# One 512-column product for two weight chunks in the input projection of an attention stage

## The reference

```python
xn = rms_norm(x, norm_g[i])
proj = jnp.einsum('bsd,de->bse', xn, w_in[i])
qa, ka, va, za, qb, kb, vb, zb = jnp.split(proj, cuts, axis=-1)
# q, k: rms_norm per head of 64
# 4 differential heads: dense softmax of two scores, a = softmax(s1) - lam * softmax(s2), o = a v, rms_norm
# 8 neighbourhood heads on a 16 x 64 grid: softmax over an 8 x 16 window with a relative bias, o = p v
ya = oa * jax.nn.silu(za);  yb = ob * jax.nn.silu(zb)
y = jnp.einsum('bse,ed->bsd', jnp.concatenate([ya, yb], axis=-1), w_out[i])
```

## Time and profile before

| | |
|---|---|
| three runs | 3197.17, 3199.08, 3201.27 us |
| median | 3199.08 us |
| span of the profiled execution | 3193.0 us |
| PE busy | 3109.5 us, 97% |
| PEld busy | 2705.6 us, 85% |
| DVE busy | 2028.7 us, 64% |
| POOL busy | 1420.3 us, 44% |
| ACT busy | 1058.5 us, 33% |

### The profile page before, as it was taken

One profiled execution on the slowest core, in us unless ns is written; L12 is line 12 of the kernel. 1 busy time (PEld: TensorE's weight loads), 2 busy tenths in 40 slices (PEclk: granted clock), 3 DMA queues, 4 the chain that ended last, 5 costly groups with the idle time before them and its releaser, 6 DMA issues.

```text
span 3193.0 us, 51486 instructions
## 1 busy us (share of the span) xinstructions
PE 3109.5 (97%) x19108; PEld 2705.6 (85%) x19108; DVE 2028.7 (64%) x3766; ACT 1058.5 (33%) x2057; POOL 1420.3 (44%) x1207
## 2 busy tenths in 40 slices
PE   9999999999989999999999999999999999999998
PEld 8898989988987889888888888988889888888886
DVE  4757576665788212687777775455553777777766
ACT  3545454541124210422222221544341422222221
POOL 5434344316643334665555545411104755555534
PEclk9999999999999999999999999999999999999999
DMA  7211201143112112111111111000002011111111
GB/s 199 75 56 38 67 28 54 38 172 97 67 34 63 52 45 68 38 59 47 53 53 53 53 53 63 7 21 17 18 21 93 27 53 53 53 53 53 53 52 53
DMA packets 181828, 179.58 MB, mean 56 GB/s; under 512 B 50234, under 2 KB 163066, under 8 KB 181498
## 3 DMA queue, kind: packets, MB, share of 16 engines
q1 hardware_dynamic: 181566, 177.02, 17.4%
q10 hardware_dynamic: 96, 0.26, 0.0%
HBM read 160.12 MB, written 22.38 MB: 57 GB/s over the span
## 4 chain that ended last, share of the span: by engine, by line
PE 63%; DVE 2%; issue 1%; ACT 1%; POOL 0%; POOLq 0%; DVEq 0%; ACTq 0%
PE banks L2692 16%; PE banks L79 13%; PE banks L81 13%; PE banks L80 13%; PE banks L3509 2%; PE banks L3486 1%; PE banks L215 1%; PE banks L3443 0%; PE banks L3444 0%; PE banks L3425 0%; POOL x L183 0%; PE banks L3452 0%; PE banks L2314 0%; DVE x L2929 0%; POOL rstd L178 0%
## 5 line engine op out<-in xcount | busy, mean ns | idle before, releaser
L2929 DVE TENSOR_TENSOR x<-x,banks 128x512 f32<-128x512 f32 x784 | 523.2, 687 | 242.2 <-PE banks L2692 233.7
L79 PE MATMUL banks<-winbuf_hi,xt_hi 128*128 128x256 f32 x1024 | 302.2, 295 | 11.7 <-ACT qkn L933 5.5
L80 PE MATMUL banks<-winbuf_lo,xt_hi 128*128 128x256 f32 x1024 | 290.0, 283 | 0.0
L81 PE MATMUL banks<-winbuf_hi,xt_lo 128*128 128x256 f32 x1024 | 290.0, 283 | 0.0
L79 PEld LDWEIGHTS banks<-winbuf_hi,xt_hi 128*128 128x128 f32 x1024 | 196.1, 191 | 33.5 <-issue 13.0
L79 PE MATMUL banks<-h1t_hi,f1w_buf_hi 128*128 128x512 f32 x512 | 199.5, 390 | 1.6 <-issue 1.6
L79 PE MATMUL banks<-h3t_hi,f2w_buf_hi 128*128 128x512 f32 x512 | 199.5, 390 | 1.6 <-issue 1.6
L81 PE MATMUL banks<-h3t_hi,f2w_buf_lo 128*128 128x512 f32 x512 | 199.2, 389 | 0.0
L81 PE MATMUL banks<-h1t_hi,f1w_buf_lo 128*128 128x512 f32 x512 | 199.2, 389 | 0.0
L80 PE MATMUL banks<-h1t_lo,f1w_buf_hi 128*128 128x512 f32 x512 | 199.2, 389 | 0.0
L80 PE MATMUL banks<-h3t_lo,f2w_buf_hi 128*128 128x512 f32 x512 | 199.2, 389 | 0.0
(11 more groups left out here) (545 smaller groups left out, 9339.6 us busy)
## 6 DMA issues: line engine op xcount, KB each, us to landing
f1w_raw<-in_w_ff SPq DMA_DIRECT2D x32, 1024.0 KB, 5.1
f2w_raw<-in_w_ff SPq DMA_DIRECT2D x32, 1024.0 KB, 5.1
winraw<-in_w_in SPq DMA_DIRECT2D x128, 128.0 KB, 3.3
gluw_raw<-in_ssm_w_glu SPq DMA_DIRECT2D x14, 512.0 KB, 4.6
x<-in_x SPq DMA_DIRECT2D x8, 512.0 KB, 6.3
wow_raw<-in_w_out SPq DMA_DIRECT2D x4, 1024.0 KB, 5.9
x<-in_x SPq DMA_DIRECT2D x1, 4096.0 KB, 15.2
gew_raw<-in_w_ple_gate SPq DMA_DIRECT2D x4, 1024.0 KB, 4.8
```

The costliest lines, as they stand in the source:

```text
L79: nc.tensor.matmul(out, a.hi, b.hi, start=start, stop=False)
L80: nc.tensor.matmul(out, a.hi, b.lo, start=False, stop=False)
L81: return nc.tensor.matmul(out, a.lo, b.hi, start=False, stop=stop)
L2929: nc.vector.tensor_tensor(xx, xx, chip.ps[:, 4 + 2 * (p % 2) + g, :], ALU.add).then_inc(s_acc, 1)
```

## The change

Two chunks can now go through one product of 512 columns into the whole of bank 6: the moving operand takes one 256-column row from each of two buffers, the output is two halves. The list `ROUNDS` says which chunks and which token tile a round has. There are 72 rounds: 8 single ones of chunk 0, 4 of chunk 1 (tiles 0 to 3), 4 pairs of chunks 1 and 2 (tiles 4 to 7), and one round for each step of units 0 to 6: for t below 4 the pair (2u + 2, 2u + 3), from t = 4 on the pair (2u + 3, 2u + 4); in unit 6 the last four are chunk 15 alone. So the heads of a unit are projected four tiles earlier than its values.

In a step the first projection is gone; the round stands where the second one was, between `scores(g + 2)` and `values(g)`. At t = 7 `scores(g + 1)` moves behind `transposes(g)`. On ACT `taken` takes both halves; it moves behind `down(g + 2)` and the second exp, and `squares(g)` moves with it behind both. The head sums, roots and scales, before eight tiles in steps 0 to 3, come one per step, three tiles ahead. There are three weight buffers instead of two, and no `winraw` of its own: the raw chunk lands in the low half of its pair and is split there in place. The next load of a buffer waits for the last round that reads it. Half of the unnormalised heads of odd units get a place of their own.

```diff
+    ROUNDS = [((0,), j) for j in range(NT)] + [((1,), j) for j in range(4)] + [((1, 2), j) for j in range(4, NT)]
+    for u in range(NU - 1):
+        for t in range(NT):
+            pair = (2 * u + 2, 2 * u + 3) if t < 4 else (2 * u + 3, 2 * u + 4)
+            ROUNDS.append((tuple(c for c in pair if c < 2 * NU), t))
+    def pair_rows(cs, k):
+        a, b = sorted(c % 3 for c in cs)
+        hi = m.win_hi[:, 16 * a + k:16 * b + k + 1:16 * (b - a), :]
+        first, last = (Mixers.LOWS[n] - Mixers.LOWS[0] + k for n in (a, b))
+        return Pair(hi, m.win_lo[:, first:last + 1:last - first, :])
...
+            def weights(c):
+                if c >= 2 * NU:
+                    return
+                if c >= 3:
+                    sp.wait_ge(s_p, last_round(c - 3) + 1)
+                for piece in range(4):
+                    for h, col in enumerate(columns(c)):
+                        sp.dma_start(m.raw[c % 3][:, 2 * piece:2 * piece + 2, h * P:h * P + P],
+                                     w_in[:, 2 * piece:2 * piece + 2, col:col + P]).then_inc(s_win[c % 3][piece], 16)
...
             for u in range(NU):
                 for t in range(NT):
-                    g, n = NT * u + t, 2 * NT * (u + 1) + 2 * t
+                    g = NT * u + t
                     more = u < NU - 1
-                    if more:
-                        project(n)
-                        if t == 7:
-                            scores(g + 1)
-                    elif t < 7:
+                    if not more and t < 7:
                         keep_going(t, 3)
-                    else:
+                    elif not more:
                         begin_output(0)
                     transposes(g)
                     if t < 6:
                         scores(g + 2)
                     if more:
-                        project(n + 1)
+                        if t == 7:
+                            scores(g + 1)
+                        project(PROLOGUE + g)
...
+            def taken(r):
+                cs, j = ROUNDS[r]
+                act.wait_ge(s_p, r + 1)
+                for c in sorted(cs):
+                    src = banked(cs, c) if len(cs) == 2 else chip.ps[:, 6, 0:CH]
+                    (values_taken if c % 2 else heads_taken)(c // 2, j, src)
...
                     more = u < NU - 1
-                    if more:
-                        taken(n)
                     evacuate(g)
...
                     if t < 7:
-                        if more:
-                            taken(n + 1)
                         if t == 1 and u and UNITS[u - 1][0] == "D":
                             out_hi(u - 1, 1)
                         if t == 4 and UNITS[u][0] == "D":
                             out_hi(u, 0)
                         if t < 6:
                             expo(g + 2, 0)
+                            down(g + 2)
+                            expo(g + 2, 1)
+                        if more:
+                            taken(PROLOGUE + g)
                         squares(g)
                         if more and t in (5, 6):
                             head_hi(u + 1, 2 * (t - 5))
                             head_hi(u + 1, 2 * (t - 5) + 1)
-                        if t < 6:
-                            down(g + 2)
-                            expo(g + 2, 1)
...
+            head_sums(NT)
+            head_sums(NT + 1)
+            head_scale(NT)
+            head_sums(NT + 2)
+            head_scale(NT + 1)
             biased(0)
+            head_scale(NT + 2)
             combine(0)
             biased(1)
```

More of the change, by code:

```diff
@@ L447, in stage_mixers @@
         s_xin = sems(nc, ctx, "mxx", " ".join(str(j) for j in range(NT)))
-        s_win = sems(nc, ctx, "mxw", "0 1 2 3")
+        s_win = [sems(nc, ctx, f"mxw{b}", "0 1 2 3") for b in range(3)]
         s_sst = sems(nc, ctx, "mxst", "0 1 2 3")
@@ L512, in _ @@
             sp.dma_start(m.xgain[:, :], row_bcast(io["norm_g"])).then_inc(s_xg, 16)
-            for piece in range(4):
-                weights(piece)
+            weights(0)
             for j in range(1, NT):
@@ L527, in _ @@
             sp.dma_start(io["s_rpb"], m.wide[:, :]).then_inc(s_wide, 16)
-            for piece in range(4, 8):
-                weights(piece)
+            weights(1)
             sp.wait_ge(s_bv, 4)
@@ L533, in _ @@
             spread_strip(sp, 0)
-            for piece in range(8, 12):
-                weights(piece)
+            weights(2)
             strips(0)
+            weights(3)
             sp.wait_ge(s_wide, 16)
@@ L542, in _ @@
             for u in range(NU - 1):
-                for t in range(4):
-                    weights(4 * (2 * u + 3) + t)
+                weights(2 * u + 4)
                 if u:
@@ L548, in _ @@
                     edges(0)
+                weights(2 * u + 5)
                 if u < NU - 2:
-                    for t in range(4):
-                        weights(4 * (2 * u + 4) + t)
                     sp.wait_ge(s_add, 2 * (NT * u + NT))
                     (strips if UNITS[u][0] == "D" else edges)(UNITS[u][1] + 1)
-            sp.wait_ge(s_p, 2 * NT * NU)
+            sp.wait_ge(s_p, len(ROUNDS))
             sp.wait_ge(s_split, 8 * NU)
@@ L1239, in _ @@
                         finish(g - 1)
-                    if more and t < 4:
+                    if a < NT * NU:
                         head_sums(a)
-                    if more and 1 <= t <= 4:
-                        head_scale(a - 1)
                     if more and t == 7:
@@ L1268, in _ @@
                             gated(u, 0)
-                    if more and t < 4:
+                    if a < NT * NU:
                         head_scale(a)
-                        head_sums(a + 1)
                     if dense:
```

127 lines of the change are left out of this document (74 added, 53 removed).

## The result

| | before | after |
|---|---|---|
| median | 3198.12 us (4 runs, 3196.95 to 3201.27) | 3286.55 us (4 runs, 3285.94 to 3287.31) |
| ratio | | 1.0278, 95% interval 1.0264 to 1.0293 |
| span of the profiled execution | 3193.0 us | 3285.1 us |
| TensorE's mean granted clock | 0.994 | 0.984 |
| standstills of PE over 1 us, 60 to 900 us | 9, together 16.9 us | 39, together 89.4 us |

What follows compares the result with a forecast made beforehand. PE's own order was taken to set the end, others counting only where PE stands. Prologue 9.4, N units 18.6 and D units 8.0 gave +36.0 on a 3193.0 span, 3229.0; plus 6.1, 3235 us; range 3212 to 3258.

Steps and rivals of the forecast that it cites:

- the mechanism: PE's loop steps: score transposes (T) lose the 2.9 us projection ahead of them, so their unchanged waits become bare.
- the N unit's standstills: Grid (N) units 1, 3, 5: PE stands before the transposes; +6.2 us per unit, +18.6 in all.
- what costs nothing: Weight splits, weight DMAs, in-place buffers, loads and head sums, roots and scales: forecast to add nothing.
- the ring: Dense (D) units: finish, combine, bias, exp, down, exp, taking, squares, variance, root, finish; 10.3 to 10.8 us against PE's 9.85.
- the width: Projection: one 512-column matmul instead of two 256-column ones saves 13.5 ns per pair, 18.1 us in all.
- those of 1 us left the clock at 1.00: Argument against the clock falling after PE's standstills, a part of rival 2.
- Rival 2: 3255 us: ring at its upper value costs each D unit 5 more, or the clock goes down, +6.5 to +34; chance 0.16.
- so four steps hide it: D units: the ring may fall behind, since combine(g+1) is needed only some 4.6 us after it is done.
- The D unit: Dense units: 89.4 us against 87.19 for units 2 and 4, +2.2 each; all D units together +8.0.
- The prologue: Before the loop and step 0: four pair rounds replace four single ones, +10.2; with the other terms +9.4 together.
- unit 0: First dense unit, from its T(1) on: 79.0 us against 74.7, +4.3.
- unit 6: Last dense unit with rounds, single from t = 4, 11.5 us less on PE: 81.4 us against 82.1, -0.7.

Runs made afterwards that it cites:

- e4: Changed kernel with each wide round split, k-tiles 0 to 3 ahead of the transposes, 4 to 7 behind the scores, and ScalarE's old order: 3178.53 us, 0.9945.
- e9: e4 with squares and head_hi on ScalarE behind both exps, the taking still early: 3211.65 us, 1.0044.
- e6: e4 with 256-column products, the first chunk's 24 ahead of the transposes, the second's 24 behind the scores: 3190.72 us, 0.9982.
- e5: Changed kernel with short groups of small filler matmuls in PE's standstills to keep the clock up: 3265.56 us, 1.0217.
- e3: Changed kernel with the round's taking, squares and head_hi of D units ahead of the second exp on ScalarE: 3267.79 us, 1.0222.
- e12: Changed kernel with e5's fillers and e3's ScalarE order together, with 8 fillers at t = 5 of D units: 3252.80 us, 1.0175.
- e7: e4 with the whole round ahead of the transposes, nothing between scores and values, and the taking ahead of evacuate: 3205.49 us, 1.0029.
- e10: e4 with the whole round ahead of the transposes in N units at t = 0 to 5 and D units at t = 0, 1, 3, 4: 3177.10 us, 0.9940.
- e11: e4 with the whole round ahead of the transposes in N units at t = 0 to 5 only: 3175.39 us, 0.9933.

## Why the prediction was right or wrong

**Right: the mechanism and the N unit's standstills.** T lost its cover, the unchanged waits became bare, and all seven units have T(6) and T(7) waiting on qklo. Forecast against measured in N units: T(2) 3.0 and 2.8, T(3) and T(4) 0.6 and 0.5, T(5) 2.2 and 2.0, T(6) and T(7) 1.9 and 1.99. e4 gives half the cover back, together with ScalarE's old order; e9, which keeps squares late, is still 75 us below the kernel after. So lost cover, with the clock that its standstills cost, is the main cause.

**Right: what costs nothing.** Buffers, loads, splits and head work cost nothing: e4 has them all and PE hardly stands. Only when the ring is late does a split hold PE up (e9).

**Right in kind: the width.** Forecast 18.1 us, measured 12.2 (e6 against e4). The 0.2257 us a wide matmul was read too low: the 443 of the window include those that overlap its ends, and between starts it is 0.2267 (441 starts in 99.73 us). By that the saving would be (0.2392 - 0.2267) x 24 x 56 = 17 us. Another part goes at the start of a group of wide matmuls, where the first distance is 0.33 us and the next four are 0.228 to 0.236 (the round from 311.95: 5.34 us over 23 distances), against 0.22 and then 0.12 in a narrow one. The transition that one projection fewer should have saved, 0.1 us a step, did not come. The rule of the Trainium skill that I had set against the rows ("TensorE: Matmul & The Clock Gate", Back-to-back issue gap) states, for a single matmul, a spacing of columns / 2.4 GHz plus about 2.5 ns; by it the change would save an estimated 3.4 us. It does not hold for these matmuls: they are 0.2267 us apart, not 0.216, and the narrow ones 0.1196, not 0.109.

**Wrong: the clock, "those of 1 us left the clock at 1.00".** I knew a drop after 3.54 us and no drop after 1.12, and most of the forecast's standstills are of 1.9 to 3 us, between the two. I put them with the short ones, without a reason. The trace of the kernel before had the warning behind the mixers: PE's standstill of 2.24 us ending at 1053.62 (L2314) was followed by 3.4 us at half clock, one of 2.05 us ending at 1031.44 was not:

```profile
1054.47:1057.88 3.41, 3.41 (x14) 3.12 (x13) 2.67 (x4) 2.13 (x4) 0.00 (x0) 0.50 0.97 272
```

The drop did come: 16 stretches, six of them behind one of the 13 standstills of 2.0 us. My own price of 1.6 us per drop was right (1.5 in N units); the number of drops was the error. e5 measures 21 us. Rival 2 held this cause at +6.5 to +34 and the ring at 5 us per D unit, but gave them as alternatives ("or the clock goes down") and at 0.16. Both happened.

**Wrong: the ring, "so four steps hide it".** The working had the right members, sized them at 10.3 to 10.8 us, and then counted on 4.6 us of slack. A turn measured 11.5 us (squares at 347.15 and 358.62): from `finish` (349.24) to the bias (353.01) it takes 3.8 us and not at most 3.3. The D unit, measured from T(0) in unit 2:

| | forecast | after | e5 (clock kept) |
|---|---|---|---|
| T(0) to T(4) | 39.9 | 45.5 | 45.5 |
| to T(5) | 12.8 | 13.1 | 13.2 |
| to T(6) | 15.5 | 16.8 | 16.8 |
| to T(7) | 11.1 | 13.8 | 11.2 |
| to the next unit | 10.1 | 10.2 | 10.2 |
| unit | 89.4 | 99.4 | 96.8 |

The slack did not last to t = 4. In the first four steps PE stands for 1.61 us (S at t = 0), 1.26 (T(2)), 0.58 and 1.52 (S and the round at t = 3), 5.0 of the 5.6 us missed. T(2) and the round are the ring: one exp less in it leaves 0.13 and 0.39 of them (e3), and T(2) stands for 1.16 even with cover when squares are late (e9). I had asked the ring only about combine and T. It also holds back `gated`, for which T(2) waits, and the taking, for which the round waits; both come before the wait that I looked at. S at t = 0 is not the ring but cover again: e3 leaves it at 1.63, and e9, with half a round ahead, has 0.41. S(2) comes right behind T(0) there, where a projection had given VectorE time to read the banks, and the forecast asked no S what it waits for. The 0.58 stays open. e3 and e12 show what the last exp in the ring is worth (18.8 us, and 15.2 in the D units with the clock kept), e9 what late squares cost on a kernel with cover (33 us).

**Small terms.** The prologue to T(0) took 12.7 us more, against 10.5 in the forecast's terms without step 0. A step of an N unit takes 9.4 us without its standing (t = 3: 9.88 less 0.48), not 9.2; 9.2 is reached only in e7, e10 and e11, where no round stands between S and V. That makes 1.6 of the 2.1 us by which N units exceed the forecast even in e5 (86.8 against 84.7). The 6.1 us that the forecast put between the span and the median as launch and end were the difference of two executions: within one execution it is 1.8 us (3286.93 and 3285.1). The forecast of the difference does not hang on it.

**The sum.** Against the forecast the measured +92.1 of span has 56.1 us more: N units 16.9, units 2 and 4 together 20.2, unit 0 7.4, unit 6 6.7, prologue 2.2, unit 7 and behind it 2.7. By cause, the clock is some 21 (e5). In e5 34.4 of span are left over the forecast: units 2 and 4 14.8, unit 6 6.7, unit 0 3.4, N units 6.3, the rest 3.2. Of these the ring's one exp makes 15.2 (e12 against e5), and S at t = 0 of units 2, 4 and 6 makes 4.9 (1.6 each). With the 6.3 of the N units that leaves 8. How much of this is the ring too stays open: e3 and e12 take out one of its members, not all, and e9 was measured with cover.

## What to carry to other kernels

When two pieces of work that each cover a wait are merged, the merged one covers one wait; if it is an accumulation it can be cut again where the waits are, in k and not in columns, with the bank left open, which here, with ScalarE's old order, turned +2.8% into -0.6% (e4). Lay out what each released wait stands for from the row in which the cover is missing (here the last unit showed it), and ask of a chain over several engines that is a little longer than a step (here the ring) what each of its members holds back, not only its last. Count each standstill from the shortest that a row shows to be harmless as one that may also cost clock.

## What the runs showed of the hardware

- The clock went to half (1.2 GHz) after standstills of 2.0 us (row at 249.31), for 3.4 us, 6.8 behind the longest; but not after each: the 2.81 us one at 218.08, the 2.40 us one at 344.55 and seven of the 13 of 2.0 us were followed by full speed. I can't say from these traces which it will be. In the kernel before, a standstill of 2.24 us (ending at 1053.62) was followed by half clock too.
- A float32 matmul of 128 columns (`stay_awake`, L87) is recorded as two, 0.112 us apart: 17 calls are the row of 34 (e5).
- A moving operand in two pieces of 256 columns costs nothing that shows: from the twelfth of a group on such 512-column matmuls start 0.226 to 0.227 us apart (the round from 311.95, and e11's), as those in one piece do (0.2267).
- An accumulation over 24 matmuls may stay open in its bank while other groups run in other banks: e4 has it in all 56 steps with a round, and a step without standing is as long as with the round whole (D, t = 2: 9.94 and 9.93 us).
- VectorE's `combine` (128 x 1024, L1199) took 1.28 us in some steps and 2.40 in others (row at 350.68), a part of the ring that changes from step to step.
